# Weighted sums of two pairs of heads in one visit of TensorE with the scores of two later pairs

## The reference, cut to what matters

```python
def fox_attention(q, k, v, log_f):            # "FoX": 32 heads, each with its own k and v
    c = cumsum(log_f)
    for each block of 128 queries:
        s = q @ k.T * 64**-0.5 + c[query] - c[key]
        s = where(key <= query, s, -1e30)
        y = softmax(s).astype(v.dtype) @ v

def swa_attention(q, k, v, sinks):            # "SWA": 8 query heads share one k and v
    for each block of 128 queries, keys in a window of 128:
        s = where(mask, q @ k.T * 64**-0.5, -1e30)
        m = maximum(s.max(), sink)
        e = exp(s - m)
        y = (e / (e.sum() + exp(sink - m))) @ v

x = x + (y * silu(gate)) @ w_out              # after each of the two
```

## Time and profile before

| | us |
|---|---|
| median of 3 runs | 2135.71 |
| lowest and highest | 2135.26 to 2136.79 |
| the profiled execution | 2136.29 |
| its span in the trace | 2134.5 |
| TensorE busy | 2119.7 |
| DVE busy | 1615.8 |
| ACT busy | 1325.8 |

### The profile page before, as it was taken

How to read it: one execution, slowest core, us unless ns; L and a number is a source line. 1 busy time by engine, 2 the same in 40 slices (tenths; PEclk the granted TensorE clock), 3 DMA queues, 4 the chain that set the end, 5 groups by cost and what they waited for, 6 DMA issues and landing times.

```text
span 2134.5 us, 34503 instructions
## 1 busy us (share of the span) xinstructions
PE 2119.7 (99%) x13406; PEld 1852.0 (87%) x13406; DVE 1615.8 (76%) x2945; ACT 1325.8 (62%) x2601; POOL 9.7 (0%) x22
## 2 busy tenths in 40 slices
PE   9999999999999999999999999999999999999998
PEld 8888888888898888888888888888888888988887
DVE  7898766787688888656888867777686777698774
ACT  6866446775576666544666666555556655567764
POOL 0000000000000000000000000000000000000000
PEclk9999999999999999999999999999999999999999
DMA  7544434565465555555555555555555565554464
GB/s 273 168 152 135 153 112 146 188 239 195 158 196 190 193 193 196 197 191 194 195 192 195 190 196 188 206 170 195 183 181 176 166 200 192 193 163 151 148 207 138
DMA packets 107619, 389.31 MB, mean 182 GB/s; under 512 B 12304, under 2 KB 12560, under 8 KB 106688
## 3 DMA queue, kind: packets, MB, share of 16 engines
q1 hardware_dynamic: 105264, 377.31, 53.1%
q0 software_dynamic: 1904, 9.47, 1.2%
q10 hardware_dynamic: 288, 0.32, 0.0%
HBM read 384.34 MB, written 2.13 MB: 181 GB/s over the span
## 4 chain that ended last, share of the span: by engine, by line
PE 92%; DVE 4%; ACT 2%; issue 1%; DMA 0%; SPq 0%; DVEq 0%; ACTq 0%
PE main L564 85%; PE two L564 5%; DVE W L1041 1%; PE two L567 1%; DVE gt L1041 1%; ACT L1708 0%; DVE GK L1047 0%; ACT W L1709 0%; DMA RAW<-ws 0%; ACT NT L1709 0%; DVE PB L1041 0%; DVE GV L1047 0%; DVE GQ L1047 0%; PE main L611 0%; ACT PP L1709 0%
## 5 line engine op out<-in xcount | busy, mean ns | idle before, releaser
L1709 ACT ACTIVATE W<-RAW 128x512 fp32r<-128x512 f32 x1416 | 881.1, 629 | 623.8 <-PE main L564 620.5
L564 PE MATMUL main<-A,W 128*128 128x256 f32 (+1 forms) x7264 | 1256.2, 333 | 3.0 <-DVE W L1041 3.0
L1041 DVE TENSOR_TENSOR W<-RAW,W 128x512 fp32r<-128x512 f32 x1416 | 960.3, 687 | 359.8 <-ACT W L1709 351.3
L564 PEld LDWEIGHTS main<-A,W 128*128 128x128 f32 x7264 | 1096.7, 188 | 154.9 <-issue 8.5
L564 PE MATMUL main<-H,W 128*128 128x512 f32 (+1 forms) x1408 | 239.7, 333 | 0.0
L564 PEld LDWEIGHTS main<-H,W 128*128 128x128 f32 x1408 | 212.2, 188 | 27.4
L564 PE MATMUL main<-B,W 128*128 128x512 f32 (+1 forms) x1216 | 197.0, 324 | 0.0
L564 PEld LDWEIGHTS main<-B,W 128*128 128x128 f32 x1216 | 176.3, 188 | 20.2
L564 PE MATMUL main<-W,A 128*128 128x512 f32 (+1 forms) x672 | 150.2, 378 | 0.0
L564 PEld LDWEIGHTS main<-W,A 128*128 128x128 f32 x672 | 117.8, 188 | 22.1 <-DVE W L1041 0.5
L564 PE MATMUL main<-W,B 128*128 128x512 f32 x384 | 88.4, 390 | 0.0
(11 more groups left out here) (308 smaller groups left out, 1379.5 us busy)
## 6 DMA issues: line engine op xcount, KB each, us to landing
RAW<-ws SPq DMA_DIRECT2D x707, 512.0 KB, 3.3
CB<-cscr POOLq DMA_DIRECT2D x4, 1024.0 KB, 5.0
XT<-xT POOLq DMA_DIRECT2D x4, 512.0 KB, 5.8
MS<-memT POOLq DMA_DIRECT2D x4, 512.0 KB, 8.2
xs<-xT SPq DMA_DIRECT2D x7, 256.0 KB, 8.3
out<-YT SPq DMA_DIRECT2D x7, 256.0 KB, 2.6
CST<-cst SPq DMA_DIRECT2D x1, 1248.0 KB, 7.0
G<-g POOLq DMA_DIRECT2D x1, 1024.0 KB, 6.8
```

Of the source, the lines that this page charges most:

```text
L564: return e.matmul(o, l, r, start=start, stop=True, skip_group_check=True)
L1041: return e.tensor_tensor(o, a, b, op)
L1709: return e.activation(o, i, f, bias=bias, scale=scale, accum_out=accum)
```

## The change

FoX pairs 2 and 3 of a group start 24 ticks after pairs 0 and 1, not 22. The sums of a FoX pair come ten ticks after its turn, at tick 24, not four; those of an SWA pair seven ticks after its turn, at tick 22, not five. At these ticks later pairs of the same banks have their scores, and the list's order puts the sums first. The sums no longer lie in columns 0 to 255 of the first bank: the 128 queries of the first block lie in the last 128 columns of the first bank, those of the second block in the last 128 columns of the second, which the scores (columns 0 to 383) leave free. For that `weigh` has three matmuls a head in place of two. The waits follow: scores no longer wait for the copy to `Y`; the sums wait for the copy of the pair before; ACT copies `Y` only when the scores of the same visit are in, and DVE reads those scores only after that copy. The copy takes two pieces of 128 columns from two banks in one instruction.

```diff
-T_FOX = [[END[f"fv{g}"] + 2 + 22 * (p // 2) for p in range(4)] for g in range(4)]
+T_FOX = [[END[f"fv{g}"] + 2 + 24 * (p // 2) for p in range(4)] for g in range(4)]
...
-            def weigh(b, v, cols, P):
+            def weigh(two, v, cols, P):
                 for h in range(2):
                     O = slice(64 * h, 64 * h + 64)
-                    mm(b[O, 0:256], v[:, 0, cols[h]], P[:, h, 0:256])
-                    z = mm(b[O, 128:256], v[:, 1, cols[h]], P[:, h, 256:384], start=False)
+                    mm(two[0][O, 384:512], v[:, 0, cols[h]], P[:, h, 0:128])
+                    mm(two[1][O, 384:512], v[:, 0, cols[h]], P[:, h, 128:256])
+                    z = mm(two[1][O, 384:512], v[:, 1, cols[h]], P[:, h, 256:384], start=False)
                 return z
...
             def fox(g, p):                                   # TensorE
-                if 4 * g + p >= 2:
-                    w.wait_ge(y_done, 4 * g + p - 1)
...
-                yield from ticks(4)
+                yield from ticks(10 - BEHIND + 2)
                 w.wait_ge(fp_ac[lane], F_AC * i + 2)
+                if 4 * g + p >= 2:
+                    w.wait_ge(y_done, 4 * g + p - 1)
...
             def swa(g, p):                                   # TensorE
                 if m >= 4:
-                    w.wait_ge(y_done, 16 + m - 3)
+                    w.wait_ge(wp_ve[lane], W_VE * i)
+                    w.wait_ge(wp_ac[lane], W_AC * i)
...
                 if m < 14:
                     w.wait_ge(wp_ve[(m + 2) % SWA_LANES], W_VE * ((m + 2) // SWA_LANES) + 1)
+                else:
+                    w.wait_ge(y_done, 16 + m - 1)
                 w.wait_ge(wp_ac[lane], W_AC * i + 2)
                 turn(PPw[lane], two, 2).then_inc(wp_pe[lane], 1)
-                yield from ticks(5)
+                yield from ticks(7)
...
+                if m >= 2:
+                    w.wait_ge(y_done, 16 + m - 1)
...
             def fox(g, p):                                   # DVE
                 w.wait_ge(fp_pe[lane], F_PE * i + 1)
+                if 4 * g + p >= 2:
+                    w.wait_ge(y_done, 4 * g + p - 1)
...
             def swa(g, p):                                   # DVE
                 w.wait_ge(wp_pe[lane], F_PE * i + 1)
+                if m >= 4:
+                    w.wait_ge(y_done, 16 + m - 3)
...
             def fox(g, p):                                   # ACT
-                yield from ticks(4)
-                w.wait_ge(fp_pe[lane], F_PE * i + 3)
-                copy(Y[:, 4 * g + p, :], two_[0][:, 0:256]).then_inc(y_done, 1)
+                yield from ticks(10)
+                w.wait_ge(fp_pe[lane], F_PE * i + (4 if i < 7 else 3))
+                copy(halfs(Y[:, 4 * g + p, :]), twos[lane][:, :, 384:512]).then_inc(y_done, 1)
...
             def swa(g, p):                                   # ACT
-                yield from ticks(3)
-                w.wait_ge(wp_pe[lane], F_PE * i + 3)
+                yield from ticks(5)
+                w.wait_ge(wp_pe[lane], F_PE * i + (4 if m < 12 else 3))
                 if m == 12:
                     w.wait_ge(rp_done, len(ROPED))
-                copy(Y[:, m, :], bank[:, 0:256]).then_inc(y_done, 1)
+                copy(halfs(Y[:, m, :]), twos[m % 2][:, :, 384:512]).then_inc(y_done, 1)
```

More of the change, by code:

```diff
@@ L981, in fox @@
                 turn(PP[lane], two).then_inc(fp_pe[lane], 1)
-                yield from ticks(4)
+                yield from ticks(10 - BEHIND + 2)
                 w.wait_ge(fp_ac[lane], F_AC * i + 2)
+                if 4 * g + p >= 2:
+                    w.wait_ge(y_done, 4 * g + p - 1)
                 cols = [slice(64 * (2 * p + h), 64 * (2 * p + h) + 64) for h in range(2)]
-                weigh(two[0], AV[d], cols, PT[lane]).then_inc(fp_pe[lane], 1)
+                weigh(two, AV[d], cols, PT[lane]).then_inc(fp_pe[lane], 1)
             def swa(g, p):
@@ L1005, in swa @@
                     w.wait_ge(wp_ve[(m + 2) % SWA_LANES], W_VE * ((m + 2) // SWA_LANES) + 1)
+                else:
+                    w.wait_ge(y_done, 16 + m - 1)
                 w.wait_ge(wp_ac[lane], W_AC * i + 2)
                 turn(PPw[lane], two, 2).then_inc(wp_pe[lane], 1)
-                yield from ticks(5)
+                yield from ticks(7)
                 w.wait_ge(wp_ve[lane], W_VE * i + 4)
                 w.wait_ge(wp_ac[lane], W_AC * i + 3)
+                if m >= 2:
+                    w.wait_ge(y_done, 16 + m - 1)
                 cols = [slice(64 * g, 64 * g + 64)] * 2
-                weigh(two[0], WV, cols, PTw[m % 2]).then_inc(wp_pe[lane], 1)
+                weigh(two, WV, cols, PTw[m % 2]).then_inc(wp_pe[lane], 1)
             w.wait_ge(s_warm, 1)
@@ L2023, in fox @@
                 lane, i = p % 2, 2 * g + p // 2
-                two_ = banks[4 + 2 * lane], banks[5 + 2 * lane]
                 mx, dn = (SM[:, 8 + 24 * lane + 4 * k:12 + 24 * lane + 4 * k] for k in range(2))
@@ L2038, in swa @@
                 lane, i = m % SWA_LANES, m // SWA_LANES
-                S, bank = PPw[lane], banks[4 + 2 * (m % 2)]
+                S = PPw[lane]
                 mx, dn, sk = (SM[:, 8 + 24 * lane + 4 * k:12 + 24 * lane + 4 * k] for k in range(3))
```

## The result

The changed kernel takes 2139.3 us (median; 2138.15 to 2140.19), the kernel before 2135.77 in the same comparison (2135.26 to 2136.79). The ratio is 1.0016, with a 95% interval of 1.001 to 1.0023: slower by 3.5 us, inside the band of 0.2% and just inside the forecast's range, but 2.7 above its 2136.6 and 0.8 above the likeliest case's own range (to 2138.5). The profiled execution took 2139.27, with a span of 2137.5.

A forecast was written before the change was run, and what follows sets the result against it. TensorE was taken as the bound nearly everywhere, hardly waiting. Visits saved -2.6, three matmuls +3.2 and the stall +0.3 gave +0.9 us: 2136.6 on the median's scale, likeliest range 2135.0 to 2138.5, whole range 2132.2 to 2139.5.

The forecast's parts named there:

- the likeliest case: Whole kernel: the summed terms give 2136.6 us, own range 2135.0 to 2138.5, chance 0.60.
- 13 visits saved: TensorE, FoX and SWA: sums share 13 scores' visits, saving entry, exit and slow start less a shape change: -2.6 us.
- sums in three matmuls: TensorE's visits of sums: head 1 starts late behind head 0's six records, +0.20 a visit, +3.2 us over 16.
- gate of group 3: FoX group 3, DVE waiting for ACT's SiLU: TensorE's stall grows to 1.4 from 0.9 to 1.1, +0.3 us.
- other waits: ACT's copies and DVE's reads at shared visits: DVE starts some 0.45 later, covered by low halves made ahead, cost 0.
- Rival C: Shared visits: changing array shape costs 0.31, so sharing saves nothing; 2139.2 us, chance 0.08.
- the upper bound of 0.22: Visits of sums: most that three matmuls a head could add per visit, in a range from -0.04.
- Rival A: Visits of sums: both heads run side by side, nothing holds head 1 back; 2132.8 us, chance 0.20.
- waits of the largest main group near 3.3: Profile after: expected waits, in us, of TensorE's largest group of main matmuls, against 3.0 before.
- Rival B: SWA: DVE becomes the bound, each of 6 shared visits stalls TensorE by 0.6; 2140.7 us, chance 0.12.
- the lead of 1.0: SWA: DVE's estimated lead of 2.7 us, of which 1.0 is left as TensorE reaches a shared visit 1.72 sooner.

The follow-up runs named there:

- three matmuls unshared: Kernel before, each head's sums written as three matmuls of 128 columns in the old columns and visits, nothing shared: 2140.46 us, ratio 1.0020.
- the copies earlier: Changed kernel with ACT's copies of the SWA sums one tick earlier in ACT's order: 2137.20 us, ratio 1.0005.

## Where the prediction held and where it failed

| term | forecast | measured | from |
|---|---|---|---|
| 13 visits saved | -2.6 | -3.6 | change against three matmuls unshared (-1.16), less the two stalls below |
| sums in three matmuls | +3.2 | +4.6 | three matmuls unshared against before |
| gate of group 3 | +0.3 | +0.60 | traces of before and after |
| other waits | 0 | +1.86 | traces; gone with the copies earlier |
| sum | +0.9 | +3.4 | |

All four are differences of the ends of main's halves from half 935 on, each between single executions.

That the time lies inside the forecast's range, by 0.2, is partly luck: three terms came out dearer than forecast, by 3.6 together, and the saved visits made up for 1.0 of that. With the forecast 2.6 saved, the change would have stood near 2140.3.

*Visits saved: right, too small.* The switch of shape inside a visit took 0.09 against the 0.11 of the earlier trace rows. TensorE's timeline of the change from 1432.80 to 1433.011:

```profile
1432.53 0.55 PE L564 MATMUL two<-PT,AV 128*64 128x128 f32 x4
1433.01 0.37 PE L564 MATMUL two<-AK,FQ 64*128 64x128 f32 x1
```

The last of the sums' records, 0.27 long as in the earlier trace rows, starts at 1432.53 + 0.55 - 0.27 = 1432.81, and the scores 0.20 later, of which 0.11 are its own. That makes 0.31 - 0.09 = 0.22 a visit. The runs give 0.26 to 0.28; the rest lies in the main halves behind the visits and wasn't traced further. Rival C (sharing saves nothing) is refuted. The Trainium skill, in TensorEngine Tiling (Array Packing), Tiling Modes, says that a change of tiling mode drains TensorE; the 0.09 agrees.

*Three matmuls: the mechanism right, the size at 0.285 instead of 0.20.* Head 1 comes 0.27 late, as worked out, and the visit alone grew by 0.23, just over the upper bound of 0.22. The 0.05 behind it weren't in the sum. Rival A is refuted as the change stands, and is what happens once the program issues the heads in turn. The Trainium skill, in TensorE: Matmul & The Clock Gate, Part 3 under The mechanism, gives TensorE a reorder window of 64, for weight loads that go to other rows of the array or to the buffer behind the running weights. The two heads here differ in columns, and six records in front of head 1 were enough to hold it; the prediction took that rule to decide for rival A, and it doesn't.

*The gate: the stall right, its cost too small.* The forecast stall of 1.4 is 1.43, but by the ends of the halves it costs 0.60 more than the one before, not 0.3. An idle time counts from the modelled end of the last record: from start to start main loses 1.59 here, and 1.12 in the kernel before. Main's first half behind the stall is also slow by 0.13, a fresh start that the step had left out.

*"Cost 0" for the waits: the step that failed.* I priced DVE's new wait as one copy and two semaphore steps, 0.45, and looked for what is queued behind the waiting engines, but not for what stands ahead of the copy in ACT's order. At one of the six shared SWA visits the copies fall into the tick in which ACT first makes the low copy of a finished block, and that copy waits for the half after the visit. A wait of one engine on another thus became a wait for TensorE itself: against TensorE's return DVE's read comes 2.8 later than in the kernel before, not 0.45, and 1.86 of it reach TensorE, not 0. The listing of ACT's order at the tick of each visit (T + 1 against the ends of the wide blocks) would have shown it: 1279 is the only one that coincides. The text's own sign, waits of the largest main group near 3.3, came out at 5.2, of which 0.3 more than before lie ahead of FoX.

*Rival B: half right.* TensorE did wait at a shared SWA visit, and the lead of 1.0 that I gave DVE there fits that one: DVE loses 2.8 (in the kernel before, its read came 0.15 ahead of TensorE's return), and 1.86 reach TensorE. But its mechanism, a busy DVE at all six, is wrong: in another shared visit of the change DVE's read comes 1.7 us behind TensorE's return and nothing stalls.

Timelines of TensorE and DVE, the first visit in the kernel before:

```profile
1909.36 0.95 DVE L1041 TENSOR_TENSOR PPw<-two,CST 128x768 f32<-128x768 f32 x1
...
1909.51 5.74 PE L564 MATMUL main<-A,W 128*128 128x512 f32 x32
```

The other visit, in the change:

```profile
1950.75 5.73 PE L564 MATMUL main<-A,W 128*128 128x512 f32 x32
...
1952.47 0.96 DVE L1048 TENSOR_TENSOR PPw<-two,CST 128x768 f32<-128x768 f32 x1 [1.25 <-ACT Y L1720]
```

## What to carry to other kernels

Where two streams use two halves of TensorE's array, issue them in turn: here the same twelve matmuls were 4.1 us dearer over 16 visits when each head was written out whole. When an edit adds a wait on another engine's instruction, read what stands ahead of that instruction in that engine's order, tick by tick; a step that is harmless at five visits held DVE for 2.7 us at the other one. Split a wait that a page gives for the whole run by where it lies, before it is laid to an edit: here 0.9 to 2.9 us of it stood ahead of all that was changed. And a saving of 3.4 us can be real and still vanish: the change was faster than the kernel before, clear of the noise, only once the order of heads and copies was mended with it.

## What the runs showed of the hardware

In these runs a record of the second half of the array starts ahead of earlier records of the first half, and all starts looked at fit one limit, that no more than three of these still wait: 0.27 us late with six in front, at once with four, and 0.11 late with four that wait behind a running pair. Changing the shape of the tiles between 128x64 and 64x128 within a visit left a gap of 0.09 us. Splitting a matmul of 256 columns into two of 128 with the same values loaded twice cost nothing that a visit shows where the heads alternate (1.46 against 1.45). A short stall of TensorE cost more than the idle time that the profile gives: 1.43 us of waiting at the gate gave back 1.7 when it went, of which 0.16 is that idle time counts from a modelled end, and 0.13 a slow first half of main.
